# Expert weights in a ring of 33 half granules, and the gathered columns fetched from DRAM by DMA

## What is computed

```python
def moe_swiglu(h, w_router, wg, wu, wd):
    logits = (h @ w_router).astype(jnp.float32)
    top_v, top_i = lax.top_k(logits, TOP_K)
    top_p = jax.nn.softmax(top_v, axis=-1)
    gates = jnp.sum(jax.nn.one_hot(top_i, N_EXPERTS, dtype=jnp.float32) * top_p[..., None], axis=-2)
    act = jax.nn.silu(jnp.einsum('bnd,edf->bnef', h, wg)) * jnp.einsum('bnd,edf->bnef', h, wu)
    act = act * gates.astype(h.dtype)[..., None]
    return jnp.einsum('bnef,efd->bnd', act, wd)
```

## Time and profile before

| | |
|---|---|
| time, median of 3 runs (lowest, highest) | 1752.54 us (1752.37, 1757.84) |
| profiled execution, own time | 1752.99 us |
| profiled execution, span from first to last instruction | 1751.2 us |
| granted TensorE clock over the span | 0.947 |
| busy share of PE / DVE / ACT / POOL | 89% / 44% / 33% / 4% |
| bytes read from HBM, written to it | 400.64 MB, 11.53 MB |
| the expert stage in the profile | about 876 to 1715 us of the span |

### The profile page before, as it was taken

The page is one execution under the profiler, slowest core; times in us unless marked ns, Lnnn a source line. Parts: engine busy times, 40 slices in busy tenths (PEclk is TensorE's granted clock), DMA queues, the critical chain, the costliest instruction groups (busy, mean ns, idle before and its releaser), DMA issues.

```text
span 1751.2 us, 24750 instructions
## 1 busy us (share of the span) xinstructions
PE 1560.6 (89%) x9147; PEld 1030.0 (59%) x9148; DVE 767.1 (44%) x1243; ACT 583.8 (33%) x994; POOL 75.9 (4%) x92
## 2 busy tenths in 40 slices
PE   4798989999999898989687999899998999999771
PEld 1684577888887585567522566545654677676220
DVE  0574676333333573766700455334453443333015
ACT  1433445233331542441200544334443333333001
POOL 2010011000000010020000000000000000000002
PEclk8899999999999899999898999999999999999885
DMA  9245536343243445465389999999999477777992
GB/s 340 97 144 169 193 110 216 119 144 117 100 144 122 144 143 188 169 207 195 108 313 389 355 388 362 388 350 360 317 371 369 173 265 262 254 270 261 395 370 80
DMA packets 202174, 414.09 MB, mean 236 GB/s; under 512 B 11336, under 2 KB 52296, under 8 KB 202032
## 3 DMA queue, kind: packets, MB, share of 16 engines
q1 hardware_dynamic: 195712, 390.64, 62.0%
q0 software_dynamic: 5264, 18.04, 3.2%
q10 hardware_dynamic: 1056, 3.54, 0.5%
HBM read 400.64 MB, written 11.53 MB: 235 GB/s over the span
## 4 chain that ended last, share of the span: by engine, by line
PE 75%; DMA 8%; DVE 6%; issue 4%; ACT 3%; SPq 2%; ACTq 1%; POOL 0%; DVEq 0%; POOLq 0%
PE ps L1966 27%; PE ps L2368 5%; PE ps L2285 5%; PE ps L2362 4%; PE ps L2286 4%; PE ps L2289 4%; DMA qkv<-in_w_moe_up 3%; PE ps L2408 3%; PE ps L2414 3%; PE ps L1898 2%; PE ps L2310 2%; DMA gu_ring<-in_w_moe_up 2%; PE ps L2313 2%; PE ps L2316 2%; SPq L679 2%
## 5 line engine op out<-in xcount | busy, mean ns | idle before, releaser
L1966 PE MATMUL ps<-d_ring_parts,scratch_parts 128*128 128x512 f32 (+1 forms) x444 | 172.4, 388 | 14.3 <-DVE hT_parts L1241 9.5
L1800 DVE TENSOR_TENSOR cst<-cst,ps 128x256 f32<-128x256 f32 (+2 forms) x89 | 32.9, 369 | 270.8 <-ACT cst L1098 270.8
L1966 PE MATMUL ps<-gu_ring_parts,scratch_parts 128*128 128x512 f32 (+1 forms) x336 | 128.0, 381 | 0.0
L1966 PE MATMUL ps<-d_ring_parts,hT_parts 128*128 128x512 f32 (+1 forms) x312 | 118.4, 380 | 0.0
L1966 PE MATMUL ps<-gu_ring_parts,o_parts 128*128 128x512 f32 x264 | 103.8, 393 | 0.0
L1966 PEld LDWEIGHTS ps<-d_ring_parts,scratch_parts 128*128 128x128 f32 x444 | 84.6, 190 | 32.5 <-issue 9.3
L2362 PE MATMUL ps<-gu_ring,hT 128*64 128x512 f32 x288 | 74.8, 665 | 30.1 <-issue 18.5
L1106 ACT ACTIVATE cst<-ps 128x128 f32<-128x128 f32 (+1 forms) x51 | 16.1, 316 | 235.4 <-PE ps L2384 221.3
L1757 DVE TENSOR_TENSOR gu_ring_parts<-gu_ring,qkv_parts 128x1024 fp32r<-128x1024 f32 x54 | 64.3, 1223 | 64.8 <-PE ps L2368 23.4
L1098 ACT ACTIVATE cst<-ps 128x256 f32<-128x256 f32 (+2 forms) x89 | 30.7, 345 | 166.3 <-PE ps L2289 74.8
L2285 PE MATMUL ps<-qkv_parts,o_parts 128*128 128x512 f32 x182 | 75.5, 415 | 4.0 <-DVE gu_ring_parts L1757 4.0
(11 more groups left out here) (414 smaller groups left out, 3369.5 us busy)
## 6 DMA issues: line engine op xcount, KB each, us to landing
gu_ring<-in_w_ada SPq DMA_DIRECT2D x48, 1024.0 KB, 7.4
gu_ring<-in_w_moe_gate SPq DMA_DIRECT2D x96, 512.0 KB, 7.9
gu_ring<-in_w_moe_up SPq DMA_DIRECT2D x96, 512.0 KB, 9.4
gu_ring<-in_w_moe_down SPq DMA_DIRECT2D x96, 512.0 KB, 9.2
d_ring<-in_w_moe_gate SPq DMA_DIRECT2D x48, 512.0 KB, 9.4
d_ring<-in_w_moe_up SPq DMA_DIRECT2D x48, 512.0 KB, 10.4
d_ring<-in_w_moe_down SPq DMA_DIRECT2D x48, 512.0 KB, 7.1
gu_ring<-in_w_in SPq DMA_DIRECT2D x16, 1024.0 KB, 7.4
```

Of the source, the lines that this page charges most:

```text
L1966: ins = pe.matmul(out, a, w, start=(start and n == 0), stop=(stop and n == 2))
```

## The change

1. The ring is now one run of 33 halves of a granule (0.5 MB each), 16.5 granules. It lies over `cache_a`, `gate2_rows`, `gu_ring`, `d_ring`, all of `scratch`, and the front of `qkv`. Granule n takes the halves 2n % 33 and (2n+1) % 33. SP waits for granule n - 16 in place of n - 11. Each granule of an expert has its own `ring_landed` semaphore.
2. `scratch` is now weights, so `hT_all` can't stay. SP stores it to the DRAM tensor `h_columns` in two DMAs (the columns of the two halves of the gather, 8 x 496 and 8 x 656 fp32 in each partition, 4.7 MB together). Each body's columns are fetched by three DMAs on ACT's queue (`fetch_columns`: 128, 192 and 64 columns for each of 8 x 128 rows, so 1024 pieces each of 512, 768 and 256 bytes, 1.57 MB). The first body's columns are still copied by ACT and DVE. In a pair, base and rest are fetched once the first expert's last step has been through PE, and part after the second's last step; in a single body all three after its last step. The copies and the readings of the table by ACT and DVE at a body's end go.
3. SP loads granules 1 to 9 first, then 0 (its place is that of `cache_a` and `gate2_rows`), then stores the columns, loads granule 15, and loads 10 to 14 (in `scratch`) once the columns are stored and the first body's copies are made.
4. The last norm's rows are loaded into the ring (the halves of granule 17) during the last body, after the early rows have been fetched.

```diff
-RING = 11
+HALVES = 33
+AHEAD = 16
...
+def half_view(buffers, pos, r):
+
+    at = (2 * (pos % GRANULES) + r) % HALVES
+    return buffers[:, D * at:D * at + D]
...
-        ln_par_end = [cache_a[:, :, :].rearrange("p a d -> p (a d)"), gate2_rows[:, :, :].rearrange("p a d -> p (a d)")]
+        ln_par_end = [half_view(ring, 17, 0), half_view(ring, 17, 1)]
...
             sp.wait_ge(out_mm, 12)
-            for pos in range(RING):
-                if pos == 9:
-                    sp.wait_ge(gather_mm, 16)
+            for pos in range(1, 10):
+                load_granule((0, 0), pos)
+            sp.wait_ge(ada_expanded, 32)
+            load_granule((0, 0), 0)
+            for first, last, n in ((0, HALF_SLOTS, 4), (HALF_SLOTS, SLOTS_PADDED, 8)):
+                sp.wait_ge(gather_act, n)
+                sp.wait_ge(gather_dve, n)
+                if n == 8:
+                    sp.wait_ge(slots_cleared, 1)
+                sp.dma_start(h_columns[:, :, first:last], hT_all[:, :, first:last]).then_inc(columns_stored, 16)
+            sp.wait_ge(gather_mm, 16)
+            load_granule((0, 0), AHEAD - 1)
+            sp.wait_ge(columns_stored, 32)
+            sp.wait_ge(hT_base, 16)
+            sp.wait_ge(hT_rest, 16)
+            sp.wait_ge(hT_part, 16)
+            for pos in range(10, AHEAD - 1):
                 load_granule((0, 0), pos)
...
-                for pos in range(RING, GRANULES):
-                    freed(t, pos - RING)
+                for pos in range(AHEAD, GRANULES):
+                    freed(t, pos - AHEAD)
                     load_granule(now, pos)
...
-                    load_ln(1, 1)
             pool.wait_ge(rows_placed, 1)
             pool.wait_ge(rows_out, STORES * NE)
...
+            pool.wait_ge(gu_freed, (NE - 1) * GU_GRANULES + granule_of(18)[3] + 1)
+            pool.wait_ge(d_freed, (NE - 1) * D_GRANULES + granule_of(17)[3] + 1)
+            load_ln(1, 1)
             pool.wait_ge(rows_out, STORES * (NE + 1))
...
-            def columns(base, rest, part):
-
-                act.activation(hT[:, 0:4, 0:P], hT_all[:, 0:4, bass.ds(base, P)], ACT.Copy).then_inc(hTg_act, 1)
-                act.activation(hT[:, 0:4, P:WIDEST], hT_all[:, 0:4, bass.ds(rest, WIDEST - P)], ACT.Copy)
-                act.activation(hT[:, 0:4, WIDEST:TOKENS], hT_all[:, 0:4, bass.ds(part, TOKENS - WIDEST)],
-                               ACT.Copy).then_inc(hTg_rest_act, 1)
+            COLUMNS = [(T_BASE, 0, P, hT_base), (T_REST, P, WIDEST - P, hT_rest), (T_PART, WIDEST, TOKENS - WIDEST, hT_part)]
+
+            def fetch_columns(t, which):
+
+                for at, c0, w, landed in which:
+                    first = act.value_load(sched[0:1, bass.ds(t + at, 1)], min_val=0, max_val=SLOTS_PADDED - w)
+                    act.dma_start(hT[:, :, c0:c0 + w], h_columns[:, :, bass.ds(first, w)]).then_inc(landed, 16)
...
                         silu_step(k)
+                        if partner and k in last_of:
+                            which = COLUMNS[2:] if last_of[k] else COLUMNS[:2]
+                            for _, _, _, landed in which:
+                                act.wait_ge(gu_mm, s0 + (k + 1)).then_inc(landed, 16)
+                            fetch_columns(t + turns, which)
                         for i in ahead[len(early):]:
                             split_high(i)
-                columns(*places)
+                if not partner:
+                    with act.If(t < NE - 1):
+                        fetch_columns(t + turns, COLUMNS)
...
                 if ng == 0:
-                    pe.wait_ge(hTg_act, t + 1)
-                    pe.wait_ge(hTg_dve, t + 1)
+                    pe.wait_ge(hT_base, t * 16 + 16)
...
                     if k == 1:
-                        pe.wait_ge(hTg_rest_act, t + 1)
-                        pe.wait_ge(hTg_rest_dve, t + 1)
+                        pe.wait_ge(hT_rest, t * 16 + 16)
+                        pe.wait_ge(hT_part, t * 16 + 16)
```

More of the change, by code:

```diff
@@ L492, in build @@
         slots_cleared = sem("slots_cleared")
-        ring_landed = [sem(f"ring_landed{k}") for k in range(RING)]
+        ring_landed = [sem(f"ring_landed{k}") for k in range(GRANULES)]
         gu_freed = sem("gu_freed")
         d_freed = sem("d_freed")
-        hTg_act = sem("hTg_act")
-        hTg_dve = sem("hTg_dve")
-        hTg_rest_act = sem("hTg_rest_act")
-        hTg_rest_dve = sem("hTg_rest_dve")
+        columns_stored = sem("columns_stored")
+        hT_base = sem("hT_base")
+        hT_rest = sem("hT_rest")
+        hT_part = sem("hT_part")
         y_mm = sem("y_mm")
@@ L674, in load_granule @@
                 e = experts[sc % 2 if sc < NSUPER - 1 else 0]
-                dst, landed = ring[pos % RING], ring_landed[pos % RING]
+                landed = ring_landed[pos]
                 if kind == "gu":
@@ L684, in load_granule @@
                         r0 = FS * sc + FC * q + P * f
-                        sp.dma_start(dst[:, D * f:D * f + D], w_moe_down[0, e][r0:r0 + P, :]).then_inc(landed, 16)
+                        sp.dma_start(half_view(ring, pos, f), w_moe_down[0, e][r0:r0 + P, :]).then_inc(landed, 16)
             def freed(t, pos):
@@ L1072, in _ @@
                     act.wait_ge(gather_dve, 4)
-                    columns(0, P, WIDEST)
+                    act.activation(hT[:, 0:4, 0:P], hT_all[:, 0:4, 0:P], ACT.Copy).then_inc(hT_base, 8)
+                    act.activation(hT[:, 0:4, P:WIDEST], hT_all[:, 0:4, P:WIDEST], ACT.Copy).then_inc(hT_rest, 8)
+                    act.activation(hT[:, 0:4, WIDEST:TOKENS], hT_all[:, 0:4, WIDEST:TOKENS], ACT.Copy).then_inc(hT_part, 8)
                 act.wait_ge(gather_mm, m + 1)
@@ L1127, in subs_before @@
                     return [i for i, sub in enumerate(subs) if sub[1] == k]
+                last_of = {max(k for k, step in enumerate(steps) if blocks[step[3]][3] == role): role for role in range(turns)}
+                act.wait_ge(columns_stored, 32)
                 if not subs:
@@ L2396, in down_of @@
                         landed(pos)
[L2397 removed]
+                        wt = half_view(ring, pos, r)
                         st, sp_ = k in starts and f == fs[0], k in ends and f == fs[-1]
```

113 lines of the change are left out of this document (55 added, 58 removed).

## The result

The changed kernel takes 1743.66 us (median of 7 runs, 1734.8 to 1747.47). The kernel before takes 1759.3 beside it (7 runs); the ratio is 0.9916, 95% interval 0.9889 to 0.9943, that is 14.8 us less. The forecast was 1739 us, 13.5 less than the 1752.54 of the first three runs of before; over all seven its median is 7 us higher, so the two changes are what to compare: 13.5 and 14.8 us. Its terms did not fare so well: a gain and a cost were both far too small, and the two errors cancelled out.

A forecast was written before the change was run, and what follows sets the result against it. It took the first and last expert bodies to wait for weights, the second to be on the edge, the third and fourth to be PE-bound; -1.5 us for the first four and -12 for the last gave 1739 us, range 1727 to 1753.

The forecast's parts named there:

- Where PE waits: Expert bodies: PE waits for weights 9.6 us in the first, at least 6.7 in the second, 16.1 in the last.
- Of the 9.6 us in A about 7 go: First expert body: granule 16 lands 7 us earlier, so about 7 of 9.6 us of PE's waits for weights go.
- The price of a fetch: Fetch of one body's columns: its small pieces take 6.0 us of all DMA engines, extrapolated from larger packets.
- an estimate of 4.7: Column fetch by the skill's 512-byte rule: 4.7 us in place of 6.0, the end 3 us earlier.
- of the nearest packets seen: Column fetch priced at 50 ns per piece (about 1 KB): 9.6 us; rival of 9.5 to 11, or last body without gain, 0.17.
- PE and what follows it are 4 us late: Change from first to second body: base lands at 964 to 965, PE now starts at 960.75, so 4 us late.
- B ends 2 us earlier than now: Second body: fewer weight waits outweigh the fetches, so it ends 2 us earlier; the third gives 1 back.
- A to D: First four expert bodies together: 1.5 us less.
- Base and rest are fetched two supers (some 40 us) before the end: Pairs of bodies: base and rest fetched some 40 us before the end, part a step before, so PE waits for none.
- E: Last expert body: five more granules in SBUF at its start, waits shrink from 16.1 to about 4 us, -12 us.
- After the last landing all stays, 44 us: End of the kernel: last steps, store, fetch and norm after the last weights land stay at 44 us.
- The -22 us that I gave a change without fetches: Rival for the expert bodies: columns cost nothing, slipping into holes; -22 us, 1731 us, chance 0.18.

The follow-up runs named there:

- nofetch: Changed kernel with no column fetches; ACT and VectorE copy other data into `hT` instead, so outputs are wrong; 1716.42 us, ratio 0.9773.
- spare: Changed kernel with the second body's columns fetched during the first body into an unused tile, then copied to `hT` at its end; 1743.08 us, ratio 0.9924.
- noln: Changed kernel without the load of the last norm's rows into the ring; 1742.68 us, ratio 0.9915.
- wide: Changed kernel with columns laid out as (column, k), so a fetch moves the same bytes in an eighth of the pieces; 1742.30 us, ratio 0.9933.
- halves: Changed kernel with each column fetch cut into two DMAs of half the columns, same bytes in twice the pieces; 1799.04 us, ratio 1.0244.
- again_c: Changed kernel run once more without edits, beside the kernels with larger pieces; 1745.56 us, ratio 0.9950.
- before_placed: Kernel before with its tiles put into SBUF in the changed kernel's order, nothing else; 1751.79 us, ratio 0.9985.

## Why the prediction was right, and by which steps

The total was right. Under it one step failed and several sizes were off, and they cancelled out; the steps in their order:

**Where PE waits** was read rightly, the size was too large: in A 6.1 of 9.6 us are left, in E 9.6 of 16.1. "Of the 9.6 us in A about 7 go": 3.5 went. The lead was smaller than put. The second store of columns was issued at 868.9 and landed after 10.4 us, at 879.3 and not at 876.4, and only then could granules 10 to 14 be asked for:

```profile
879.29 2.71 SPq L723 DMA_DIRECT2D ring<-in_w_moe_down  x4
```

Granule 16, asked for from 888.1 on, landed about 10.3 us later, at 898 and not at 895, against 902 before: a lead of 4 us in place of 7. With the early start undone A's waits are 4.0 longer and A 5.9.

**The price of a fetch** held: 5.7 us of all engines against 6.0. This is the step that I had thought the weakest. (q10's share is rounded, which leaves 0.4 either way.) Short stretches, in which one size of piece passes at a time, give the same by size. From 958 to 962 us there are pieces of 512 bytes only:

```profile
q1 hardware_dynamic: 587, 1.15, 80.0%
q10 hardware_dynamic: 584, 0.30, 27.5%
```

Share x 16 x length / packets makes 30 ns for 512 bytes here, 40 for 768 (966 to 970 us) and 19 for 256 (974 to 978), beside the line's 31, 41 and 22, and 87 for q1's 2 KB. The rule of the Trainium skill ("DMA: Bandwidth & Descriptors", Specifications), by which 512 and 768 bytes go at the full rate and less than 512 does not, gave an estimate of 4.7. This case does not agree with it: at q1's 2 KB price for a byte, 512 and 768 bytes would take 23 and 34 ns, and 256 bytes show no jump. (The prediction's 50 ns "of the nearest packets seen" is the line's value at 1 KB; the nearest row has 57 ns, at 1.2 KB.)

**"PE and what follows it are 4 us late"** came true as a number: A, from its start to B's, is 4.4 us longer. That is luck, since two errors stand behind it. I took base to be issued where ACT's copies stood, at 956.5, and to land 8 us later; it was issued at 953.08 and PE was let go 13.3 us later. And PE was to wait 3 to 5 us and waited 17.2: it had no work from 949.2 on and reached the end of A 11 us sooner than before (960.1). I had left PE at its old time, although 7 us saved in A had been counted already.

Of these 11 us, 5.5 I had not seen. In before PE waited that long for ACT's last product of A, for which PE's part was done at 951.2:

```profile
956.68 3.41 PE L2408 MATMUL ps<-qkv,cst 128*64 128x512 f32 x8 [5.51 <-ACT cst L1106]
```

ACT stood still from 951.2 to 956.3 with no release shown. In after it stands still about as long, but behind that product and ahead of the fetch (947.3 to 952.9), so that 3.8 of PE's 17.2 us pass before the fetch is issued at all. The DMA records show a candidate for the cause: in each pause one packet of 8 KB of q14, a queue of the kind "instruction", passes the saturated engines, at 954.8 in before and 951.3 in after, and ACT goes on 1.2 us after it. So ACT may wait there for its own next instructions. No run tries it.

Rest came at 974, not 970, and part at 982, which cost PE 6.4 more. In `nofetch` A is 15.4 us shorter. So the first fetch took all that A had gained, and 4 us more.

**"B ends 2 us earlier than now"** is the step that failed. B was to start 4 us late and still end early, so to be 6 us shorter, C 1 longer. Measured: B 0.7 shorter, C 0.8 longer. The weights did come in time, as foreseen: in B all of PE's waits for them are gone (3.5 and 3.2 us, and 0.7 more). But 6.4 us of waiting for part took their place, which I had not looked at, and the first 16 matmuls of B lost 2.5 us to the lower clock after PE's pause (9.58 in place of 7.13). This is 5.3 of the 7.4 us by which A to D missed the forecast (+5.9 against -1.5). D makes up most of the others: it grew by 1.4, and PE's pause between D and E, with no release shown, is 11.2 us in place of 8.4. `spare` shows what bounds C: what PE gains ahead of it, it waits for weights there.

**"Base and rest are fetched two supers (some 40 us) before the end"** had a wrong number. For C they are issued 19 us ahead of its first matmul; base lands 6 us ahead of it, rest 2 us behind. PE waits 1.3 us for columns in C and 1.2 in D. It cost little.

**E** gained 9.9 against 12. At its start 240 granules had landed in place of 236, 3.5 more with those in part: not five. What the norm's rows cost, 2.6 by forecast, `noln` can't tell from nothing.

**"After the last landing all stays, 44 us"** was wrong by 5 in our favour: 38.8. Before, ACT stood idle ahead of its last product, with no release shown, and PE for it; the chain in before, then in after:

```profile
1712.43 0.28 ACT L1106 ACTIVATE cst<-ps 128x128 f32<-128x128 f32 x1 [5.66 <-issue]
1712.76 2.47 PE L2408 MATMUL ps<-qkv,cst 128*64 128x512 f32 x8 [2.69 <-ACT cst L1106]
1716.26 0.56 ACTq L1175 DMA_DIRECT2D y_rows<-qkv  x1
1720.68 0.94 POOL L812 DMA_INDIRECT qkv<-y_rows,row_at  x1 [21.59 <-DMA y_rows<-qkv]
```

```profile
1705.66 1.94 PE L2446 MATMUL ps<-ring,cst 128*64 128x512 f32 x8 [0.43 <-ACT cst L1159]
1709.59 0.60 ACTq L1231 DMA_DIRECT2D y_rows<-qkv  x1
1712.99 0.99 POOL L862 DMA_INDIRECT qkv<-y_rows,row_at  x1 [17.68 <-DMA y_rows<-qkv]
```

2.3 of the 5 us are that wait, and 2 more are work that PE still had before behind the last landing and has now done ahead of it; the store takes 3.4 from issue to the next fetch in place of 4.4. In this pause of ACT, too, a packet of q14 passes, at 1711.0. Why the stall fell elsewhere wasn't tried.

**Ahead of the experts** nothing was forecast, since the diff touches no step there. From the 1000th to the 3500th matmul 4 to 5 us went, 3 to 4 of them with the placing of the tiles.

**The sum.** E -9.9, the tail -4.9, the stage ahead -4.7, A to D +5.9: -13.6, beside -13.5 forecast and -14.8 measured on the medians. That the three agree is luck. The forecast had nothing for two of the four terms, which make 9.6 us, and had the other two too good by 2.1 and 7.4; the -4.7 is a mean over profiles of the one stretch, while no single pair of profiles gives this sum (-7.7 and -22.4 us, by their starts). Behind it stand two terms far larger than I had them: the depth is worth 26 us and the fetches cost 25. The -22 us that I gave a change without fetches would have been some -40. The price by bytes and packets was right, the price by time under way missing.

**The theory of the pieces.** By counts: a fetch has 1024 pieces, 64 for each engine. If each waits its turn behind one packet of the weights (395.35 MB in 197,792 packets, 2.0 KB, some 87 ns by the line), base takes 64 x (31 + 87) ns = 7.6 us, rest 64 x (41 + 87) = 8.2, part 64 x (22 + 87) = 7.0. Measured by who is let go: 7.6 from base to rest (966.4 to 974.0), 8.4 from rest to part, beside which q1's packets are larger (3.2 KB on average from 974 to 978 us). The remaining 5 to 6 us of base's can be divided by the DMA records: its first piece moves at 957.1, 4.0 us after the issue, its last at 965.6, and PE is let go 0.8 later. With an eighth of the pieces the landing falls by half (`wide`), with twice as many it takes 21.7 us (`halves`). The Trainium skill says the like ("DMA: Bandwidth & Descriptors", Queues, rings and completion order): an engine takes turns between the rows of queues it has work for, one packet at a time, and a packet is typically 9 to 17 descriptors. This case's trace agrees with turns but not with that length: while both queues have work, q10 and q1 pass the same number of pieces, 584 and 587 from 958 to 962 us (the rows above), 579 and 576 from 962 to 966, 544 and 545 from 966 to 970. From 958 to 966 the starts of pieces follow the ends of pieces of the other queue, 3 to 4 ns before them, and those of the same queue no more often than by chance. So a turn is one piece here, of 512 bytes as of 2 KB.

**The signs** that I named: waits in E at 5 us or less (no, 9.6), E 12 shorter (10), waits in A at 3 or less (no, 6.1), PE or ACT waiting 3 to 5 at B's start with a fetch as the releaser (no, 17.2 and 10.0), B and C within 4 (yes, by 0.1), q10 with 12,000 packets more near 31 ns (12,480, 29 ns), SP's stand in D shorter (barely): one line fell from 89.2 to 65.5, but the other rose, and both together are 118 in place of 120 us:

```profile
SPq L723 <- PE ps L2327: 65.5, 5, 24.3
SPq L717 <- PE ps L2327: 52.5, 10, 23.2
```

No measured version is better than the changed kernel by more than can be told; `nofetch` computes something else.

## What to carry to other kernels

A transfer has two prices: what it takes of the engines, and how long it is under way beside a full queue. In this case it goes by the number of its pieces more than by its bytes, as each piece waits for one of the full queue's; and an engine that issues many of them is held meanwhile. Read it from the landings of a like transfer at a like load, and set it against the time at which the consumer will be ready after the change, not before it. When a total comes out right, check the terms: here a gain of 26 us and a cost of 25 hid behind a forecast of 14. And a layout that makes a DMA's pieces large is paid for by every engine that then reads or writes with a stride.

## What the runs showed of the hardware

- Two saturated queues share the DMA engines piece by piece: from 958 to 962 us 584 pieces of 512 bytes passed beside 587 of 2 KB on average.
- Pieces of 256, 512 and 768 bytes in a saturated stream cost 19, 30 and 40 ns of an engine, with no jump below 512 bytes, but a fetch of 512 KB in 1024 of them landed after 13.9 us, in 128 pieces after 7.3.
- Issuing them holds ACT: three issues took 9.4 us (953.08), the store behind them 5.9, six issues in `halves` 33.0.
- ACT stands still for some 5 us in A with no release shown, in both kernels, and goes on 1.2 us after a packet of an instruction queue (955.1 and 951.7). That the two hang together is not shown.
- TensorE's load of a 128x128 stationary tile took 189 ns with contiguous columns and 320 to 333 ns with columns 32 bytes apart; one such load in three was nearly hidden, with three in three D took 12 us more than in `again_c`, 9 of them behind its first super. ACT's copy of 2048 elements took 1.91 and 3.92 us, VectorE's subtraction 1.58 and 2.71. The Trainium skill ("SBUF — State Buffer", Door 1: The DMA port swizzle) gives SBUF lines of 16 bytes and full rate only for two or more hits in a line; all three agree.
- The granted clock follows the pauses. In after, A stands at 0.88 and B at 0.96, against 0.91 and 0.99: after the 17 us without work PE's matmuls of B run at a granted 0.50, the lower of its two levels (1.2 GHz), until 971, and the first 16 take 9.58 us in place of 7.13. After the 6.4 us ahead of 982.3 the granted clock is 0.50 again.
- Where tiles lie in SBUF moved 530 us of work ahead of the experts by 3 to 4 us in one profile (`before_placed`), with no instruction changed.
